# Stages ahead of an expert loop in another order: row tiles in banks of their own, products by which low parts they need, group sums inside the output projection

## The chip, the cores and the metric

The kernel runs on one core of one Trainium2 chip. Its metric is the device time of one execution in microseconds. The profiled execution is one more run of the same program, read by the hardware profiler.

## The reference

One layer of a decoder on 512 tokens of 1024 numbers, all in float32. Two token mixers, an attention in a sliding window and a short convolution, share one input projection; each result is normalised on its own, both go through one output projection, and a mixture of 32 experts (four for each token) follows.

```python
h = rmsnorm(x, g_mix)
p = h @ w_in                              # 768 columns q,k,v and 1536 of the convolution
attn = sliding_window_attention(q, k, v, sinks)      # 8 heads, blocks of 128 queries
conv = short_conv(b_gate, c_gate, x_in, conv_w)      # b * (width-3 conv of c * x_in)
mix = concatenate([rmsnorm(attn, g_attn_out), rmsnorm(conv, g_conv_out)])
x = x + mix @ w_out
h = rmsnorm(x, g_ffn)
x = x + moe(h, w_router, b_router, w1, b1, w2, b2)   # top 4 of 32, softmax gates
out = rmsnorm(x, g_final)
```

## The kernel before

The order of work is written out by hand: each engine has its own list of instructions, and semaphores tie them. The 512 tokens are `TB` = 4 row tiles of 128. Four stages follow each other.

**Input.** For each row tile ScalarE takes the sum of squares (`row_std`), VectorE scales the rows (`norm`), TensorE turns them (`turn_rows`), ScalarE rounds what was turned to the short float format of TensorE (`high_xn`, into `xnT_hi`), and VectorE keeps the rest (`low_xn`, into `xnT_lo`). The row tiles use two pairs of PSUM banks in turn. Weights are split in the same way, `high_tile` on ScalarE and `low_tile` on VectorE, a tile of 128 columns at a time.

**Projection and attention.** `project(m, bank, done)` makes one of 18 column tiles, six of q, k, v and then twelve of the convolution, from 24 products: for each of eight slices `k` high x high, high weight x low rows, low weight x high rows. Between them lie the scores, the turning of the probabilities and `attend(n)` for each of four blocks. VectorE's loop over the blocks ends with `attended(n)` (L955, L957), which scales the attention output and sums its squares. The last block also prepares the output weights: `high_w_out` (ScalarE L1414) and `low_w_out` (VectorE L981), eight slices in the order `W_OUT_EARLY + W_OUT_LATE`; `high_mix` (L1421, L1422) and `low_mix` (L987, L988) split the mixed rows of one row tile.

**Output projection.** `out_proj(t, n)` takes row tile `t` and column half `n`, 24 products (L634 to L636) into two banks, one of each group. `group_sums` (L645) adds the squares of both groups over the partitions; ScalarE takes the root (L1466), VectorE the reciprocal (L1060). Only then can `residual(t, n)` (L1068, L1069) scale the banks and add them to `X`, which frees them for row tile `t + 1`. `second_norm` (L1082), `turn_h2`, `router` and `rank` follow for each row tile, one tile behind.

**Experts.** SyncE streams all the weights of the experts through a ring of 16 slots of 1 MB. The first four slots are asked for once the last `project` is done, the next four once the output projection is, the third part once the rows of the first expert were fetched (`rows_in`), and all others as slots come free. TensorE multiplies at L778, L785, L804 and L810. Then the result rows are gathered and added (L1278) and normalised.

## Time and profile before

| | us |
|---|---|
| median of 3 runs | 1254.84 |
| lowest and highest | 1253.53, 1255.98 |
| the profiled execution | 1252.27 |
| its span, first to last instruction | 1250.5 |
| TensorE busy | 1158.2 (93%) |
| VectorE, ScalarE, GpSimd busy | 309.7, 198.1, 169.9 |
| mean bytes by DMA | 368 GB/s |

Times of the trace are microseconds from the start of the span. A row of the timeline gives the start, how long, the engine, the line, the operation with what it writes and reads, and in brackets how long the engine had been idle and who released it.
### The profile page before, as it was taken

The page shows a single profiled execution, that of the slowest core. Times are in us where ns is not written, and L with a number is a line of the kernel's source. Part 1 is how long each engine was busy: PE and PEld are TensorE (multiplying, and loading weights), DVE is VectorE, ACT ScalarE, POOL GpSimd, SP SyncE. Part 2 cuts the span into 40 slices and gives each one's busy share as a digit, 9 for nine tenths or more (in the row PEclk, how much of TensorE's full clock was granted, in tenths as well). Part 3 has the DMA queues.
Part 4 walks back from the last instruction along what each step waited for, and adds up shares of the span by engine and source line. Part 5 has one row for each costly group of instructions (what it writes and reads, how often), then busy time and mean ns, then how long its engine had stood idle before and what let it go on. Part 6 is the DMA issues. An engine that isn't in the chain of part 4 may idle for free. (4 is left out here: it accounts for less than half of the span.)

```text
span 1250.5 us, 16597 instructions
## 1 busy us (share of the span) xinstructions
PE 1158.2 (93%) x7030; PEld 484.9 (39%) x7030; DVE 309.7 (25%) x470; ACT 198.1 (16%) x385; POOL 169.9 (14%) x246
## 2 busy tenths in 40 slices
PE   5999998798999999999999898999989899998980
PEld 4777677323333333333333333333333333333330
DVE  4678855411101202101101010110101011010108
ACT  4453623001001101011010000101000010100002
POOL 6000000341111201111111011111101111111000
PEclk9999989698999999999999999999999999999995
DMA  9400635999999999999999999999999999999996
GB/s 332 145 1 27 236 142 220 320 392 411 423 424 424 423 425 423 425 422 425 424 423 425 425 423 424 425 423 423 424 424 424 423 425 423 424 423 424 425 394 249
DMA packets 59246, 460.67 MB, mean 368 GB/s; under 512 B 12438, under 2 KB 12710, under 8 KB 26306
## 3 DMA queue, kind: packets, MB, share of 16 engines
q1 hardware_dynamic: 49362, 434.15, 84.0%
q0 software_dynamic: 7632, 17.05, 3.6%
q10 hardware_dynamic: 2176, 8.39, 1.7%
q8 instruction: 57, 0.93, 0.3%
q14 instruction: 19, 0.16, 0.0%
HBM read 442.58 MB, written 21.41 MB: 371 GB/s over the span
## 5 line engine op out<-in xcount | busy, mean ns | idle before, releaser
L778 PE MATMUL ps<-ring_a,blockT 128*64 128x512 f32 x1472 | 327.2, 595 | 15.6 <-DMA ring_a<-in_w 15.5
L1234 DVE TENSOR_SCALAR xnT<-ps 128x768 f32<-128x768 f32 (+1 forms) x32 | 26.9, 841 | 828.4 <-PE ps L785 520.6
L778 PEld LDWEIGHTS ps<-ring_a,blockT 128*64 128x64 f32 x1472 | 101.1, 137 | 226.8 <-issue 187.7
L804 PE MATMUL ps<-ring_a,actT 128*64 128x512 f32 x736 | 166.3, 598 | 0.0
L1497 ACT ACTIVATE blockT<-ps 128x512 f32<-128x512 f32 x30 | 17.9, 597 | 561.4 <-PE ps L730 561.4
L778 PE MATMUL ps<-ring_b,blockT 128*64 128x512 f32 x448 | 99.7, 595 | 6.7 <-DMA ring_b<-in_w 6.7
L1674 POOL DMA_INDIRECT scores<-h_rows,slots x30 | 31.7, 1058 | 509.6 <-PE ps L730 508.7
L785 PE MATMUL ps<-ring_a,blockT 128*32 128x512 f32 x768 | 87.4, 595 | 0.0
L804 PEld LDWEIGHTS ps<-ring_a,actT 128*64 128x64 f32 x736 | 50.2, 137 | 93.5 <-issue 91.0
L1690 POOL DMA_INDIRECT expert_rows<-normed,slots x32 | 32.9, 1029 | 270.1 <-ACT normed L1526 269.8
L804 PE MATMUL ps<-ring_b,actT 128*64 128x512 f32 x288 | 64.7, 596 | 0.0
L524 PE MATMUL ps<-xnT_hi,ring_r 128*128 128x512 f32 x144 | 57.8, 401 | 5.6 <-DVE ring_r L892 3.5
L778 PEld LDWEIGHTS ps<-ring_b,blockT 128*64 128x64 f32 x448 | 30.7, 137 | 71.0 <-issue 57.3
L525 PE MATMUL ps<-xnT_lo,ring_r 128*128 128x512 f32 x144 | 56.9, 395 | 0.0
L526 PE MATMUL ps<-xnT_hi,ring_r 128*128 128x512 f32 x144 | 56.8, 394 | 0.0
L810 PE MATMUL ps<-ring_a,actT 128*32 128x256 f32 x832 | 50.3, 382 | 0.0
L785 PEld LDWEIGHTS ps<-ring_a,blockT 128*32 128x32 f32 x768 | 22.5, 109 | 62.6 <-issue 62.6
L1255 DVE TENSOR_TENSOR xnT<-xnT 128x768 f32<-128x768 f32 (+1 forms) x32 | 42.7, 1334 | 9.3 <-ACT xnT L1520 8.7
L810 PEld LDWEIGHTS ps<-ring_a,actT 128*32 128x32 f32 x832 | 24.4, 109 | 34.5 <-issue 21.1
L1525 ACT ACTIVATE normed<-ps,slots 128x256 f32<-128x256 f32 x18 | 8.5, 474 | 174.5 <-PE ps L810 174.5
L1526 ACT ACTIVATE normed<-ps,slots 128x512 f32<-128x512 f32 x32 | 21.9, 684 | 81.8 <-PE ps L804 81.8
L804 PEld LDWEIGHTS ps<-ring_b,actT 128*64 128x64 f32 x288 | 20.0, 136 | 35.9 <-issue 35.0
(289 smaller groups left out, 1090.3 us busy)
## 6 DMA issues: line engine op xcount, KB each, us to landing
ring_a<-in_w SPq DMA_DIRECT2D x98, 2048.0 KB, 32.1
ring_a<-in_w SPq DMA_DIRECT2D x92, 1024.0 KB, 30.1
ring_b<-in_w SPq DMA_DIRECT2D x30, 2048.0 KB, 31.0
ring_b<-in_w SPq DMA_DIRECT2D x36, 1024.0 KB, 32.8
ring<-in_w_in SPq DMA_DIRECT2D x12, 768.0 KB, 19.2
ring<-expert_rows SPq DMA_DIRECT2D x16, 512.0 KB, 14.7
h_rows<-normed ACTq DMA_DIRECT2D x4, 1536.0 KB, 6.5
X<-in_x SPq DMA_DIRECT2D x8, 512.0 KB, 6.1
```

The lines of the kernel that those rows point to most:

```text
L524: mm(ps[:, bank, :], high[:, k, :], xnT_hi[:, k, :], start=(k == 0), stop=False)
L525: mm(ps[:, bank, :], high[:, k, :], xnT_lo[:, :, k, :], start=False, stop=False)
L526: ins = mm(ps[:, bank, :], low[:, k, :], xnT_hi[:, k, :], start=False, stop=(k == KT - 1))
L778: ins = mm(ps[half * HALF:(half + 1) * HALF, b, :], x_of(k)[0], ring(r)[:, 0, at + half * 512:at + (half + 1) * 512], start=False, stop=(k ...
L785: mm(ps[q * QUARTER:(q + 1) * QUARTER, B_BOTH, :], x_of(k)[1], w[:, :, q * 256:(q + 1) * 256], start=False, stop=(k == KT - 1), tile_posit ...
L804: ins = mm(ps[half * HALF:(half + 1) * HALF, bank, :], actT[:, s % 2 * W2_K + j, s // 2 * HALF:(s // 2 + 1) * HALF], ring(r)[:, 0, j * D + ...
L810: ins = mm(ps[q * QUARTER:(q + 1) * QUARTER, bank + 1, 0:256], actT[:, 4 + j, s * QUARTER:(s + 1) * QUARTER], ring(slot(s)[0])[:, 0, j * D ...
L1234: v.tensor_scalar(width(glu_c, big), width(ps_glu, big), LIMIT, None, ALU.min).then_inc(glu_ready, 1)
L1255: v.tensor_tensor(turned.rearrange("p (s k q) -> p s q k", k=W2_K, q=P), a_in.rearrange("p (s q k) -> p s q k", k=W2_K, q=P), b_in.rearran ...
L1526: a.activation(gated_y[:, parity, 0:512], ps[:, bank, :], ACT.Copy, scale=gates[:, HALVES, 1:2].bitcast(F32)).then_inc(y_ready, 1)
L1674: g.indirect_dma_start(gathered[:, 0:512], None, h2_halves, bass.IndirectOffsetOnAxis(lists[:, HALVES, 0:1], 0), bounds_check=last_half_ro ...
L1690: g.indirect_dma_start(y_halves, bass.IndirectOffsetOnAxis(slots[:, HALVES, i, 0:1], 0), gated_y[:, parity, 0:512], None, bounds_check=las ...
```

## The change

Six edits, none in the expert loop.

1. The four row tiles are turned into four pairs of banks (`2 * t` in place of `2 * (t % 2)`), and TensorE no longer waits for `xn_lo` between them. ScalarE takes the sums of squares of three row tiles before the first `high_xn`.
2. `project` waits for the high weights, makes all eight high x high products, then the eight with the low rows, and waits for the low weights only ahead of the last eight.
3. The first output tile is made by `out_first` in the same manner, for both halves; `group_sums` stands ahead of its last 16 products, those with the low weights.
4. VectorE no longer makes two low slices of `w_out` inside the last block; after the block comes `low_mix(0)`, then two slices, `attended(3)`, four slices, `low_mix(1)`.
5. The sum of the squares of the convolution over its four channel tiles goes from one reduction on VectorE (L1055) to three additions on GpSimd, each as its square arrives.
6. `out_proj` keeps the old product order for row tiles 1 to 3.

TensorE's first projected tile, in the order of the program before; `tile_lo` is told by VectorE:

```order
L506 MATMUL ps<-ident,normed 128x128 [waits xn_lo,xn_ready]
L506 MATMUL ps<-ident,normed 128x128 x7
L524 MATMUL ps<-xnT_hi,ring_r 128x512 [waits tile_lo,xn_lo]
L525 MATMUL ps<-xnT_lo,ring_r 128x512
L526 MATMUL ps<-xnT_hi,ring_r 128x512
```

The same place in the changed program:

```order
L505 MATMUL ps<-ident,normed 128x128 [waits xn_ready]
L505 MATMUL ps<-ident,normed 128x128 x7
L521 MATMUL ps<-xnT_hi,ring_r 128x512 [waits tile_hi,xn_lo,xn_hi]
L521 MATMUL ps<-xnT_hi,ring_r 128x512 x7
L525 MATMUL ps<-xnT_lo,ring_r 128x512 [waits xn_lo]
L525 MATMUL ps<-xnT_lo,ring_r 128x512 x7
L528 MATMUL ps<-xnT_hi,ring_r 128x512 [waits tile_lo]
L528 MATMUL ps<-xnT_hi,ring_r 128x512 x7
```

The wait for the low weights has moved behind sixteen products.

TensorE at the end of the first output tile, before; the three rows of products ahead of the sums are the last of 48:

```order
L634 MATMUL ps<-ring_r,xnT_hi 128x512
L635 MATMUL ps<-ring_r,xnT_hi 128x512
L636 MATMUL ps<-ring_r,mixer_r 128x512
L645 MATMUL ps<-ones_col,early 128x1 [waits csqs_ready,osqs_ready]
L645 MATMUL ps<-ones_col,early 128x1 x7
L634 MATMUL ps<-ring_r,xnT_hi 128x512 [waits x2_half,mix_lo]
```

And the whole of it in the changed program, from the last `attend`:

```order
L587 MATMUL ps<-probsT,mixer 64x256 x7
L637 MATMUL ps<-ring_r,xnT_hi 128x512 [waits mix_hi,wout_hi,conv_read,u_ready]
L637 MATMUL ps<-ring_r,xnT_hi 128x512 [waits wout_hi] x7
L642 MATMUL ps<-ring_r,mixer_r 128x512 [waits mix_lo]
L642 MATMUL ps<-ring_r,mixer_r 128x512 x7
L637 MATMUL ps<-ring_r,xnT_hi 128x512 x8
L642 MATMUL ps<-ring_r,mixer_r 128x512 x8
L670 MATMUL ps<-ones_col,early 128x1 [waits csqs_ready,osqs_ready]
L670 MATMUL ps<-ones_col,early 128x1 x3
L670 MATMUL ps<-ones_col,normed 128x1 x4
L649 MATMUL ps<-ring_r,xnT_hi 128x512 [waits wout_lo] x8
L649 MATMUL ps<-ring_r,xnT_hi 128x512 x8
```

The sums stand ahead of sixteen products where they stood behind all of them.

VectorE from the end of the last block's `attended(2)` to the first `residual`, before:

```order
L957 TENSOR_REDUCE early<-early 128x128
L981 TENSOR_TENSOR ring_r<-ring,ring_r 128x1024 [waits wout_hi] x2
L1034 TENSOR_TENSOR early<-early,ps 128x512 [waits part_done]
L1043 COPY probsT<-ps 128x512 [waits dve_step,pv_done,probs_turned]
L1046 TENSOR_SCALAR mixer<-early,g_conv 128x512
L1043 COPY probsT<-ps 128x512 [waits probs_turned]
L981 TENSOR_TENSOR ring_r<-ring,ring_r 128x1024 [waits wout_hi]
L987 TENSOR_TENSOR mixer_r<-mixer,xnT_hi 128x4x128 [waits mix_hi]
L988 TENSOR_TENSOR mixer_r<-mixer,xnT_hi 128x4x128
L981 TENSOR_TENSOR ring_r<-ring,ring_r 128x1024 [waits wout_hi] x3
L955 TENSOR_TENSOR mixer<-ps,g_attn 128x4x128 [waits osq_ready]
```

And in the changed program:

```order
L980 TENSOR_REDUCE early<-early 128x128
L1053 TENSOR_TENSOR early<-early,ps 128x512 [waits part_done]
L1062 COPY probsT<-ps 128x512 [waits dve_step,pv_done,probs_turned]
L1065 TENSOR_SCALAR mixer<-early,g_conv 128x512
L1062 COPY probsT<-ps 128x512 [waits probs_turned]
L1010 TENSOR_TENSOR mixer_r<-mixer,xnT_hi 128x4x128 [waits mix_hi]
L1011 TENSOR_TENSOR mixer_r<-mixer,xnT_hi 128x4x128
L1004 TENSOR_TENSOR ring_r<-ring,ring_r 128x1024 [waits wout_hi] x2
L978 TENSOR_TENSOR mixer<-ps,g_attn 128x4x128 [waits osq_ready]
L980 TENSOR_REDUCE early<-early 128x128
L1004 TENSOR_TENSOR ring_r<-ring,ring_r 128x1024 [waits wout_hi] x4
```

Two slices have left the place ahead of the block's last multiplication, and six are now made behind `low_mix(0)`. The diff, cut to its core:

```diff
-                if t >= 2:
-                    pe.wait_ge(xn_lo, 2 * (t - 1))
-                turn_rows(normed[:, t % 2, :], 2 * (t % 2)).then_inc(xn_turned, 1)
+                turn_rows(normed[:, t % 2, :], 2 * t).then_inc(xn_turned, 1)
...
-                pe.wait_ge(tile_lo, m + 1)
+                pe.wait_ge(tile_hi, m + 1)
                 _, low, high = weight_tile(m)
                 for k in range(KT):
                     mm(ps[:, bank, :], high[:, k, :], xnT_hi[:, k, :], start=(k == 0), stop=False)
+                if m == 0:
+                    pe.wait_ge(xn_lo, 2 * TB)
+                for k in range(KT):
                     mm(ps[:, bank, :], high[:, k, :], xnT_lo[:, :, k, :], start=False, stop=False)
+                pe.wait_ge(tile_lo, m + 1)
+                for k in range(KT):
                     ins = mm(ps[:, bank, :], low[:, k, :], xnT_hi[:, k, :], start=False, stop=(k == KT - 1))
...
-            pe.wait_ge(xn_lo, 2 * TB)
+            pe.wait_ge(xn_hi, 2 * TB)
+            pe.wait_ge(xn_lo, 2 * (TB - 1))
...
+            def out_first():
+
+                pe.wait_ge(u_ready, CT)
+                pe.wait_ge(conv_read, CT)
+                for n in range(2):
+                    if n == 0:
+                        pe.wait_ge(mix_hi, 1)
+                    for order, k in enumerate(W_OUT_EARLY + W_OUT_LATE):
+                        if n == 0:
+                            pe.wait_ge(wout_hi, order + 1)
+                        bank, high, _, w_high, _ = out_parts(0, n, k)
+                        mm(bank, high, w_high, start=(k in (0, W_OUT_LATE[-1] + 1)), stop=False)
+                    if n == 0:
+                        pe.wait_ge(mix_lo, 1)
+                    for k in W_OUT_EARLY + W_OUT_LATE:
+                        bank, _, low, w_high, _ = out_parts(0, n, k)
+                        mm(bank, low, w_high, start=False, stop=False)
+                group_sums()
+                for n in range(2):
+                    for order, k in enumerate(W_OUT_EARLY + W_OUT_LATE):
+                        if n == 0:
+                            pe.wait_ge(wout_lo, order + 1)
+                        bank, high, _, _, w_low = out_parts(0, n, k)
+                        ins = mm(bank, high, w_low, start=False, stop=(k in (CT - 1, W_OUT_LATE[-1])))
+                    ins.then_inc(oproj_done, 1)
...
-            out_proj(0, 0)
-            out_proj(0, 1)
-            group_sums()
+            out_first()
...
-                if n == TB - 1:
-                    low_w_out(2)
-                    low_w_out(3)
-
...
-            for order in range(4, KT):
+            low_mix(0)
+            for order in range(2, KT):
                 low_w_out(order)
-                if order == 4:
-                    low_mix(0)
-            attended(TB - 1)
-            dve.wait_ge(sq_ready, CT)
-            v.tensor_reduce(conv_sqs[:, :], conv_sq.rearrange("p c t -> p t c"), AX_X, ALU.add).then_inc(csqs_ready, 1)
+                if order == 3:
+                    attended(TB - 1)
             low_mix(1)
...
-                if t >= 1:
-                    high_xn(t - 1)
-            high_xn(TB - 1)
+                if t >= 2:
+                    high_xn(t - 2)
+            for t in range(TB - 2, TB):
+                high_xn(t)
...
+            for n in range(1, CT):
+                pool.wait_ge(sq_ready, n + 1)
+                ins = g.tensor_tensor(conv_sq[:, 0, :], conv_sq[:, 0, :], conv_sq[:, n, :], ALU.add)
+                if n < CT - 1:
+                    then(ins)
+                else:
+                    ins.then_inc(csqs_ready, 1)
```

## Rows read from the trace of the kernel before

**Rows 1.** The page's 40 slices of the span: bytes moved by DMA.

```profile
GB/s 332 145 1 27 236 142 220 320 392 411 423 424 424 423 425 423 425 422 425 424 423 425 425 423 424 425 423 423 424 424 424 423 425 423 424 423 424 425 394 249
```

**Rows 2.** The windows view: stretch, length, busy time of five engines, PEclk, DMA share, GB/s.

```profile
430.00:530.00 100.00, 100.00 (x646) 34.09 (x644) 14.15 (x18) 10.08 (x19) 14.11 (x14) 1.00 1.01 424
730.00:830.00 100.00, 95.53 (x578) 31.23 (x578) 11.81 (x14) 8.98 (x17) 12.80 (x12) 1.00 1.01 424
```

**Rows 3.** Timeline of SyncE's queue: requests for experts' weights.

```profile
146.81 85.57 SPq L417 DMA_DIRECT2D ring_a<-in_w  x6
```

**Rows 4.** Timeline of TensorE where the first expert's rows have come.

```profile
231.69 1.51 PE L723 MATMUL ps<-ident,scores 96*128 96x96 f32 x8 [0.61 <-DMA scores<-h_rows,tok_static]
```

**Rows 5.** Timeline of TensorE at the first projected tile.

```profile
22.51 0.77 PE L524 MATMUL ps<-xnT_hi,ring_r 128*128 128x512 f32 x1 [3.47 <-DVE ring_r L892]
```

**Rows 6.** Timeline of ScalarE there.

```profile
19.08 1.08 ACT L1346 ACTIVATE xnT_hi<-ps 128x512 fp32r<-128x512 f32 x2 [1.59 <-PE ps L506]
20.05 2.00 ACT L1340 ACTIVATE ring_r<-ring 128x1024 fp32r<-128x1024 f32 x2
```

**Rows 7.** Timeline of VectorE there.

```profile
21.14 2.36 DVE L892 TENSOR_TENSOR ring_r<-ring,ring_r 128x1024 fp32r<-128x1024 f32 x2
```

**Rows 8.** Timeline of TensorE from the third block's attention to the second row tile.

```profile
131.14 1.95 PE L584 MATMUL ps<-probsT,mixer 128*64 128x256 f32 x16
...
144.03 1.03 PE L567 MATMUL ps<-ident,scores 128*128 128x128 f32 x8
145.32 0.66 PE L567 MATMUL ps<-ident,scores 128*128 128x128 f32 x4 [0.25 <-ACT probsT L1451]
147.46 0.66 PE L567 MATMUL ps<-ident,scores 128*128 128x128 f32 x4 [1.48 <-DVE probsT L1043]
148.94 3.35 PE L584 MATMUL ps<-probsT,mixer 128*64 128x256 f32 x16 [0.83 <-issue]
152.22 0.73 PE L634 MATMUL ps<-ring_r,xnT_hi 128*128 128x512 f32 x1
...
163.49 1.84 PE L645 MATMUL ps<-ones_col,early 128*128 128x1 f32 x16
167.59 0.77 PE L634 MATMUL ps<-ring_r,xnT_hi 128*128 128x512 f32 x1 [2.26 <-DVE X L1069]
...
175.78 1.03 PE L506 MATMUL ps<-ident,normed 128*128 128x128 f32 x8
```

**Rows 9.** The windows view in that stretch, columns as in Rows 2.

```profile
150.00:151.00 1.00, 1.00 (x8) 0.74 (x6) 1.00 (x2) 1.00 (x3) 0.00 (x0) 0.50 1.03 422
169.00:170.00 1.00, 1.00 (x4) 0.80 (x3) 0.96 (x2) 0.00 (x0) 0.00 (x0) 0.50 0.00 0
```

**Rows 10.** Timeline of VectorE in that stretch.

```profile
143.44 2.35 DVE L981 TENSOR_TENSOR ring_r<-ring,ring_r 128x1024 fp32r<-128x1024 f32 x2
145.71 0.68 DVE L1034 TENSOR_TENSOR early<-early,ps 128x512 f32<-128x512 f32 x1
148.15 0.69 DVE L1043 COPY probsT<-ps 128x512 f32<-128x512 f32 x1 [0.36 <-PE ps L567]
...
151.09 3.49 DVE L981 TENSOR_TENSOR ring_r<-ring,ring_r 128x1024 fp32r<-128x1024 f32 x3
...
156.11 3.80 DVE L1055 TENSOR_REDUCE early<-normed 128x512 f32<-128x2048 f32 x1
...
165.91 0.75 DVE L1068 SCALAR_TENSOR_TENSOR X<-ps,r_group,X 128x512 f32<-128x512 f32 x1
...
171.83 1.42 DVE L1082 SCALAR_TENSOR_TENSOR normed<-X,stat,gain_ffn 128x512 f32<-128x512 f32 x2
```

**Rows 11.** Timeline of ScalarE in that stretch.

```profile
149.10 2.93 ACT L1414 ACTIVATE ring_r<-ring 128x1024 fp32r<-128x1024 f32 x3
```

**Rows 12.** The views of single lines: GpSimd L1606, then VectorE L885.

```profile
L1606 POOL TENSOR_SCALAR ring<-ring x8: 849/852/1832, 4.3 to 12.7; 128x256 f32<-128x256 f32 x8
...
L885 DVE SCALAR_TENSOR_TENSOR normed<-X,stat,gain_a x4: 1283/1285/1285, 7.0 to 15.7; 128x1024 f32<-128x1024 f32 x4
```

More of the change, by code:

```diff
@@ L231, in layer_kernel @@
         u_pad = early[:, 3 * SEQ:]
-        conv_sqs = u_pad[:, 0:SEQ]
         upper = scores[:, HEADS // 2:, :].rearrange("p h s -> p (h s)")
@@ L613, in _, with out_parts @@
                     scores_of(n + 1, 1)
+            def out_parts(t, n, k):
+                half, c = k // CT, k % CT
+                rows, cols = slice(t * P, (t + 1) * P), slice(n * 512, (n + 1) * 512)
+                return (ps[:, 2 * n + half, :], mixT_hi[:, k, rows], (attnT_lo, convT_lo)[half][:, c, rows],
+                        w_out_hi[:, W_OUT_PLACES[k], cols], w_out_lo[:, k, cols])
+            def out_first():
[22 more added lines that the diff above has]
+                    ins.then_inc(oproj_done, 1)
@@ L616, in out_proj @@
             def out_proj(t, n):
-                if t == 0 and n == 0:
-                    pe.wait_ge(u_ready, CT)
-                if t == 0 and n == 1:
-                    pe.wait_ge(conv_read, CT)
                 if n == 0:
                     pe.wait_ge(mix_lo, t + 1)
-                if t:
-                    pe.wait_ge(x2_half, 2 * (t - 1) + n + 1)
-                cols = slice(n * 512, (n + 1) * 512)
-                for order, k in enumerate(W_OUT_EARLY + W_OUT_LATE):
-                    if t == 0 and n == 0:
-                        pe.wait_ge(wout_lo, order + 1)
-                    half, c = k // CT, k % CT
-                    bank = ps[:, 2 * n + half, :]
-                    high, low = mixT_hi[:, k, t * P:(t + 1) * P], (attnT_lo, convT_lo)[half][:, c, t * P:(t + 1) * P]
-                    w_high = w_out_hi[:, W_OUT_PLACES[k], cols]
+                pe.wait_ge(x2_half, 2 * (t - 1) + n + 1)
@@ L634, in out_proj @@
+                for k in W_OUT_EARLY + W_OUT_LATE:
+                    bank, high, low, w_high, w_low = out_parts(t, n, k)
                     mm(bank, high, w_high, start=(k in (0, W_OUT_LATE[-1] + 1)), stop=False)
-                    mm(bank, high, w_out_lo[:, k, cols], start=False, stop=False)
+                    mm(bank, high, w_low, start=False, stop=False)
                     ins = mm(bank, low, w_high, start=False, stop=(k in (CT - 1, W_OUT_LATE[-1])))
@@ L642, in group_sums @@
                 pe.wait_ge(csqs_ready, 1)
-                for half, src in enumerate((attn_sqs, conv_sqs)):
+                for half, src in enumerate((attn_sqs, conv_sq[:, 0, :])):
                     for t in range(TB):
@@ L898, in low_xn @@
                     half = slice(4 * b, 4 * b + 4)
-                    v.tensor_tensor(xnT_lo[:, t, half, :], ps[:, 2 * (t % 2) + b, :].rearrange("p (k t) -> p k t", k=4),
+                    v.tensor_tensor(xnT_lo[:, t, half, :], ps[:, 2 * t + b, :].rearrange("p (k t) -> p k t", k=4),
                                     xnT_hi[:, half, t * P:(t + 1) * P].bitcast(F32), ALU.subtract).then_inc(xn_lo, 1)
@@ L1345, in high_xn @@
                 for b in range(2):
-                    a.activation(xnT_hi[:, 4 * b:4 * b + 4, t * P:(t + 1) * P], ps[:, 2 * (t % 2) + b, :].rearrange("p (k t) -> p k t", k=4),
+                    a.activation(xnT_hi[:, 4 * b:4 * b + 4, t * P:(t + 1) * P], ps[:, 2 * t + b, :].rearrange("p (k t) -> p k t", k=4),
                                  ACT.Copy).then_inc(xn_hi, 1)
```

## The prediction

> **What bounds the kernel now.** I read the page's slices first. The DMA engines move 423 to 425 GB/s in nearly every slice from the eleventh on, and next to nothing in the third [rows 1]. The windows view of the expert loop says the same from both sides: in the stretch from 430 us TensorE is busy for all of 100 us and DMA moves 424 GB/s, in the one from 730 us TensorE is busy for 95.5 us and DMA again moves 424 GB/s [rows 2]. So the loop is a stream of weights at the full rate, and its length is its bytes over that rate. The diff touches neither. What it can move is the moment at which the stream begins. SyncE's queue asks for only the first eight slots before that: six requests for `ring_a` are spread over 85.57 us from 146.81 on, and the last two of these come after `rows_in` [rows 3]. TensorE turns the first expert's rows at 231.69, freed by the fetch of these rows [rows 4]. The fetch needs the routing of the last row tile, which comes from TensorE's own chain through the stages before. So the question is what TensorE waits for, and how fast it runs, ahead of 231.69. A microsecond saved there should be one saved at the end. I then read TensorE's timeline for gaps, and the granted clock behind each.
>
> **The start: 1.3 us.** TensorE's first projected product starts at 22.51, freed by VectorE's low weight tile after 3.47 us of idling [rows 5]. VectorE makes two such tiles in 2.36 us from 21.14 on [rows 7], so the first costs some 1.2 us plus the handing over. Its high tile is the first of two that ScalarE makes in 2.00 us from 20.05 [rows 6], done at 21.1. The changed program needs only that one: 22.51 - 21.15 = 1.36 us. The low rows of the last row tile are needed eight products later and the low weights sixteen later; both are done by 22.4, and eight products take at least 1.9 us, so these waits end unseen. The banks of their own bring nothing by themselves: the last row tile's scaling on VectorE starts at 15.7 and takes 1.285 us [rows 12], TensorE turns it, and ScalarE's copies start at 19.08 [rows 6]. VectorE has no room ahead of it, and the earlier sums of squares on ScalarE now stand ahead of the first `high_xn`. I take 0.1 us off for that (0 to 1 us lost, if the third row tile of `x` lands late, since ScalarE now waits for it ahead of `high_xn(0)`). The other bound is the pace at the start: the first product takes 0.77 us [rows 5], as does the first one at half clock later on [rows 8]. If the pace rises no earlier than before, products started 1.36 us sooner run at half pace for that long and bring 0.7. Sum: 1.3 us, between 0 and 1.4. The other seventeen tiles have the same 24 products each and no gap to win.
>
> **The end of attention.** In the last block VectorE makes two low slices of `w_out` from 143.44 on for 2.35 us, and only then, at 145.71, the product L1034 [rows 10], whose input TensorE finished by about 144.2, when it went on to turn probabilities (144.03) [rows 8]. Everything to `attend(3)` hangs on that: TensorE idles 1.48 us until 147.46, then 0.83 us until 148.94 [rows 8]. With the slices gone L1034 starts 1.5 us sooner. TensorE is free for the last turning at 145.32 + 0.66 = 145.98, so that moves from 147.46 to 146.0, and `attend(3)` from 148.94 to 147.5. It took 3.35 us there, and the same sixteen took 1.95 us one block before [rows 8]: the granted clock was 0.50 [rows 9], the lower of its two levels, after three microseconds in which TensorE had mostly idled. With 1.5 us less of idling I expect 1.00 and 1.95 us, so that it ends at 149.45 in place of about 152.2.
>
> **A new wait eats part of it.** `out_first` needs all eight high slices of `w_out` in its first eight products. ScalarE makes the last three of them from 149.10 for 2.93 us, to 152.03 [rows 11]. That chain doesn't move. Before, three products lay between two slices and hid it. Now the eighth product would start at about 151.3 and has to wait 0.8 us, until 152.1. The clock's gain of 1.4 us in `attend(3)` therefore mostly goes into this wait.
>
> **The sums in the middle: the largest term.** Before, 48 products ran from 152.22 to 163.49, 0.235 us each; then the sums took 1.84 us; then TensorE idled 2.26 us for root, reciprocal and first `residual`, and started the second row tile at 167.59 [rows 8]. After: from 152.1 on 41 products at 0.235 and the sums, 152.1 + 9.6 + 1.8 = 163.6. Sixteen products (3.8 us) lie behind the sums, and the first eight of them close the banks of half 0 at about 161.7; root and reciprocal are long done by then. `residual(0, 0)` takes two operations of 0.75 us [rows 10] and ends at 163.2, so TensorE goes on at 163.6 without a gap: 167.59 - 163.6 = 4.0 us. The 24 products of `out_proj(1, 0)` took 175.78 - 167.59 = 8.19 us [rows 8] at a granted clock of 0.50 [rows 9] over most of it. At 0.235 us they take 5.6: another 2.55 us. What is late next is `turn_h2(0)`: VectorE ended the second norm at 171.83 + 1.42 = 173.25, 7.3 us behind the start of the first `residual` at 165.91 [rows 10]. From 161.7 that gives 169.05, just ahead of TensorE at 163.6 + 5.6 = 169.2. So the turn moves from 175.78 to 169.2, 6.6 us, with nothing to spare. From there the order is the old one and the rest moves as it is.
>
> **What hides the moved work.** VectorE's chain from `low_mix(0)` on starts when ScalarE has the rows, 149.2: 1.2 us, two slices at 1.2, `attended(3)` 1.6, four slices 4.7, `low_mix(1)` 1.2, end near 160.2; one slice is a third of 3.49 [rows 10]. The last slice is ready at about 159.0 and needed at 161.5; `low_mix(1)` is done 1.5 us ahead of `residual(0, 0)`. The reduction of 3.80 us at 156.11 [rows 10] would not have fitted; it is now three additions on GpSimd. No row shows such an addition. The nearest is L1606, one input of half the length, 0.85 us undisturbed [rows 12]: twice that is the least, 1.7 us, four times the most, 3.4. The last square arrives at 147.2, so the addition ends by 150.6, and the sums need it at 158. Nothing on the path: zero, and 0.6 us at worst if it had to wait for a pause of VectorE. Queued behind it on GpSimd are only the clearing of the row buffer and small constants, needed far later.
>
> **Trace and rule.** Of L1606's eight operations some took 1.83 us in place of 0.85, beside VectorE's L885, while L885 stayed between 1.283 and 1.285 us all four times, three of them beside GpSimd's work [rows 12]. VectorE lost nothing. The Trainium skill (SBUF — State Buffer, section Who interferes with whom) says that a VectorE instruction with two SBUF inputs and a GpSimd one that reads SBUF lock each other out, whichever comes second. The trace agrees for GpSimd, not for VectorE. By that rule `low_mix(0)` could wait for the addition: a rival below.
>
> **Sum.** 1.3 + 6.6 = 7.9 us. The profiled execution took 1252.27 us, which gives 1244.4; it lies 2.57 us under the median of the runs shown. Taken from the median: 1254.84 - 7.9 = **1246.9 us**.
>
> **The rivals.** (a) *The clock stays low.* `attend(3)` still starts at 0.50 and the first products with it: 3.35 us from 147.5, then seven products at 0.43, so the eighth starts at 153.9 and not 152.1, 1.8 us lost; and the clock could fall behind the sums as it did before, now inside `out_first`, 2.55 us more, the price at that place in [rows 8]. Against it: the idling is 1.5 us shorter, and the gap behind the sums is gone. 1248.7, at most 1251.3. (b) *GpSimd holds VectorE.* The addition runs from 147.3 to 150.6, `low_mix(0)` starts 1.4 us late, all the slack of VectorE's chain goes, and the rest lands on the first `residual` and on `turn_h2(0)`: 0.4 to 1 us, 1247.6. For it is only the slowing of L1606; against it L885. (c) *Slower: the grouped products cost more each.* 432 products of the projection and 48 of the first output tile now run in groups of eight from the same kind of operand; before, kinds alternated. If the alternation hid weight loads or reads that groups don't, each costs more. From 7.9 / 480 = 16 ns each (0.235 to 0.251) the kernel is slower than before; at twice that 1262.7. Nothing in the rows speaks for a difference between the kinds. (d) *The loop doesn't pass it on.* If the stream began by something else than `rows_in`, or lost at its start what it won, the time would stay at 1254.8. Against it: the queue's rows show the requests held back until 232 [rows 3].
>
> **How the numbers follow.** Forecast 0.60, (a) 0.22, (b) 0.06, (c) 0.04, (d) 0.08. The forecast's own case spans 1244.2 (runs of one kernel differ by over 1 us to either side) to 1248.5 (no gain at the start). With (a) up to two thirds of its price the range goes to 1250.4; beyond lie (c), (d) and the tail. A difference of 0.2%, 2.5 us, is about what can be told from none. Faster by over that: forecast, (a), (b), 0.88; within it: (d), 0.08; slower: (c), 0.04.
>
> **What would show it.** In the changed profile: first projected product near 21.2 and not 22.5; no wait of the last turning of probabilities; sixteen products of `attend(3)` in 2 and not 3.4 us; a wait of some 0.8 us for ScalarE's L1414 (its new number) inside the first output tile; the second row tile started with no gap, some 5.3 us sooner, at clock 1.00; the turning of the first expert's rows near 223.8; and the loop's length from there as before. If that last moves by other than the end does, the first step of this text is wrong.

## The result, and the profile after

The changed kernel takes 1248.11 us (median of 5 runs, 1244.19 to 1248.85). The kernel before took 1255.98 us in the 5 runs beside them, the three shown above among these. The ratio is 0.9933, 95% interval 0.9919 to 0.9947: faster by 0.7%, 8.4 us (6.7 to 10.2). Two later timings of the same pair gave 0.9927 (0.991 to 0.9945) and 0.9912 (0.9899 to 0.9925). The forecast was 1246.9 us, range 1244.2 to 1250.4.

The two profiled executions lie closer together: 1252.27 us before, 1248.85 after. So these two traces hold only 3.4 us of the difference.

TensorE's timeline after, at the first projected tile and the next; the columns are as before:

```profile
20.98 3.75 PE L521 MATMUL ps<-xnT_hi,ring_r 128*128 128x512 f32 x8 [2.21 <-ACT ring_r L1357]
24.53 3.09 PE L525 MATMUL ps<-xnT_lo,ring_r 128*128 128x512 f32 x8
27.46 2.00 PE L528 MATMUL ps<-xnT_hi,ring_r 128*128 128x512 f32 x8
29.29 1.98 PE L521 MATMUL ps<-xnT_hi,ring_r 128*128 128x512 f32 x8
31.11 1.98 PE L525 MATMUL ps<-xnT_lo,ring_r 128*128 128x512 f32 x8
```

It starts 1.53 us sooner than in [rows 5] and waits for ScalarE's high tile only. But the first eight products take 3.55 us (24.53 - 20.98), 0.44 each, where the eight from 29.29 take 1.82, 0.228 each. The second tile starts at 29.29; before it started at 29.90, so 0.61 of the 1.53 us are left there.

The same view around the last block of attention and the first output tile, against [rows 8]:

```profile
145.00 1.03 PE L570 MATMUL ps<-ident,scores 128*128 128x128 f32 x8
146.28 1.32 PE L570 MATMUL ps<-ident,scores 128*128 128x128 f32 x8 [0.25 <-ACT probsT L1469]
148.44 1.95 PE L587 MATMUL ps<-probsT,mixer 128*64 128x256 f32 x16 [0.83 <-ACT probsT L1469]
...
152.03 0.50 PE L637 MATMUL ps<-ring_r,xnT_hi 128*128 128x512 f32 x1
152.97 0.50 PE L637 MATMUL ps<-ring_r,xnT_hi 128*128 128x512 f32 x1 [0.44 <-ACT ring_r L1432]
...
159.58 1.03 PE L670 MATMUL ps<-ones_col,normed 128*128 128x1 f32 x8
160.48 3.93 PE L649 MATMUL ps<-ring_r,xnT_hi 128*128 128x512 f32 x16
164.37 0.47 PE L659 MATMUL ps<-ring_r,xnT_hi 128*128 128x512 f32 x1
...
170.08 1.09 PE L505 MATMUL ps<-ident,normed 128*128 128x128 f32 x8
```

The last turning no longer waits (one row of eight in place of two of four), `attend(3)` takes 1.95 and not 3.35 us, the eighth product stands 0.94 us behind the seventh (0.7 over the usual 0.235: the new wait), and the second row tile follows at once. From the first of these rows to the last it is 25.08 us; before it was 31.75.

VectorE there, against [rows 10], and the line of GpSimd's additions:

```profile
145.20 0.69 DVE L1053 TENSOR_TENSOR early<-early,ps 128x512 f32<-128x512 f32 x1 [0.21 <-PE ps L528]
150.10 0.69 DVE L1010 TENSOR_TENSOR mixer_r<-mixer,xnT_hi 128x512 fp32r<-128x512 f32 x1 [1.77 <-ACT xnT_hi L1440]
162.68 0.75 DVE L1085 SCALAR_TENSOR_TENSOR X<-ps,r_group,X 128x512 f32<-128x512 f32 x1 [1.53 <-PE ps L649]
168.61 1.41 DVE L1099 SCALAR_TENSOR_TENSOR normed<-X,stat,gain_ffn 128x512 f32<-128x512 f32 x2
```
```profile
L1673 POOL TENSOR_TENSOR normed<-normed x3: 1277/1286/1302, 103.5 to 148.2; 128x512 f32<-128x512 f32 x3
```

VectorE has 1.53 us to spare ahead of the first `residual`. What did not go well stands elsewhere, near 60 us. The windows view there, then the turning of the first expert's rows, against [rows 4], and SyncE's queue behind it, against [rows 3]:

```profile
62.00:63.00 1.00, 1.00 (x4) 0.81 (x3) 1.00 (x2) 1.00 (x2) 0.00 (x0) 0.50 0.00 0
```
```profile
60.50 3.36 PE L521 MATMUL ps<-xnT_hi,ring_r 128*128 128x512 f32 x8 [2.17 <-DVEq L998]
...
226.11 1.51 PE L746 MATMUL ps<-ident,scores 96*128 96x96 f32 x8 [0.66 <-DMA scores<-h_rows,tok_static]
```
```profile
226.00 0.81 SPq L416 DMA_DIRECT2D ring_a<-in_w  x2
226.84 1.48 SPq L416 DMA_DIRECT2D ring_b<-in_w  x2
240.83 3.41 SPq L421 DMA_DIRECT2D ring_a<-in_w  x4
```

At 62 us the granted clock is 0.50, which the trace of before does not have there, and the 24 products from 60.50 take 7.18 us where before they took 5.59: 1.6 us lost. The rows are turned 5.58 us sooner, and the stream goes on with them.

### The profile page after: what moved, and what is told of

It reads as the page before. It is cut to its first block and busy times, and to the rows that moved or that the text cites. A ratio compares the mean times of both kernels' runs of the same rounds, so it can differ in the third digit from the quotient of the medians.

```text
span 1247.3 us, 16600 instructions
## 1 busy us (share of the span) xinstructions
PE 1159.8 (93%) x7030; PEld 483.9 (39%) x7030; DVE 306.2 (25%) x469; ACT 197.6 (16%) x385; POOL 172.3 (14%) x249
## 5 line engine op out<-in xcount | busy, mean ns | idle before, releaser
L1251 DVE TENSOR_SCALAR xnT<-ps 128x768 f32<-128x768 f32 (+1 forms) x32 | 26.9, 841 | 830.8 <-PE ps L808 522.8
L521 PE MATMUL ps<-xnT_hi,ring_r 128*128 128x512 f32 x144 | 39.6, 421 | 4.4 <-ACT ring_r L1357 2.2
L525 PE MATMUL ps<-xnT_lo,ring_r 128*128 128x512 f32 x144 | 37.1, 401 | 0.0
L528 PE MATMUL ps<-xnT_hi,ring_r 128*128 128x512 f32 x144 | 35.6, 389 | 0.0
```

The source lines that it names most:

```text
L521: mm(ps[:, bank, :], high[:, k, :], xnT_hi[:, k, :], start=(k == 0), stop=False)
L525: mm(ps[:, bank, :], high[:, k, :], xnT_lo[:, :, k, :], start=False, stop=False)
L528: ins = mm(ps[:, bank, :], low[:, k, :], xnT_hi[:, k, :], start=False, stop=(k == KT - 1))
L1251: v.tensor_scalar(width(glu_c, big), width(ps_glu, big), LIMIT, None, ALU.min).then_inc(glu_ready, 1)
```

## Where an execution spends its time

Each profiled kernel is one execution. Three distances in TensorE's timeline, and what is left to the end of the span, put all fourteen side by side (us; the last column says whether the clock fell near 60 us):

| kernel | turning of the last block's probabilities at | from there to `turn_h2(0)` | to the rows of the first expert | from there to the end | 0.50 near 60 us |
|---|---|---|---|---|---|
| before | 144.03 | 31.75 | 55.91 | 1018.8 | no |
| old_again (the kernel before) | 144.21 | 32.01 | 55.79 | 1022.3 | no |
| after | 145.00 | 25.08 | 56.03 | 1021.2 | yes |
| again (changed) | 144.84 | 25.09 | 55.82 | 1023.3 | yes |
| again_2 (changed) | 142.31 | 25.08 | 56.25 | 1022.6 | no |
| sums_last | 143.95 | 28.49 | 55.65 | 1022.4 | yes |
| slices_early | 142.68 | 29.70 | 55.84 | 1020.9 | no |
| low_first | 146.29 | 25.13 | 55.61 | 1022.5 | yes |
| squares_on_vector | 144.28 | 27.33 | 56.08 | 1022.5 | yes |
| rows_later | 142.70 | 25.09 | 61.14 | 1020.8 | no |
| rows_much_later | 144.70 | 25.09 | 67.41 | 1019.9 | yes |
| warm_start | 140.53 | 25.08 | 55.99 | 1022.2 | no |
| warm_tail | 142.36 | 25.09 | 55.21 | 1021.0 | no |
| warm_all | 140.04 | 25.09 | 55.50 | 1021.6 | no |

The second column repeats to 0.01 us in the three executions of the changed kernel. In the two of the kernel before it is 0.26 us apart: there stretches of the lower clock lie inside it, and VectorE's chain stood otherwise to TensorE's, so that the last turning waited 2.08 us in `old_again` where it waited 1.48:

```profile
148.24 0.66 PE L567 MATMUL ps<-ident,scores 128*128 128x128 f32 x4 [2.08 <-DVE probsT L1043]
```

So an edit that brings no low clock into this column can be read from one execution; one that does can't be read to better than about a microsecond. Between executions of one kernel the first column moved by up to 2.7 us, the last by up to 3.5. Three things stand behind that.

*The moment at which the clock rises at the start.* In the second control, `again_2`, TensorE's timeline has the same first product as after, but the pace is full by 24.5 and not by 26.9:

```profile
21.04 3.62 PE L521 MATMUL ps<-xnT_hi,ring_r 128*128 128x512 f32 x8 [2.21 <-ACT ring_r L1357]
24.50 2.01 PE L525 MATMUL ps<-xnT_lo,ring_r 128*128 128x512 f32 x8
...
28.16 1.98 PE L521 MATMUL ps<-xnT_hi,ring_r 128*128 128x512 f32 x8
```

The Trainium skill (TensorE: Matmul & The Clock Gate, Part 1, on the warm-up) says that the number of slow products at a kernel's start differs from run to run, because the gate's observation of activity is not tied to the program's start. The traces agree: the second tile starts at 28.16 here and at 29.29 in after.

*The fall near 60 us.* The gap ahead of it, 2.17 us for VectorE, is the same in every execution without added products ahead of it. The clock fell behind it in six of ten such executions of the changed order, in two of the three of the changed kernel itself, and in neither of the two of the kernel before. So the changed order doesn't bring the fall each time, as `again` alone could have suggested; whether it makes the fall likelier is open, since two executions of the kernel before are too few to tell. The windows view of `again_2`, where it did not:

```profile
62.00:63.00 1.00, 1.00 (x6) 0.80 (x6) 0.85 (x3) 0.98 (x2) 0.00 (x0) 1.00 0.00 0
```

*The first expert.* In `old_again`, the kernel before once more, TensorE idles three times, 3.4 us in all, inside the first expert's products, with nothing that the trace shows to wait for:

```profile
257.43 1.30 PE L785 MATMUL ps<-ring_a,rowsT 128*32 128x512 f32 x3 [0.82 <-issue]
260.25 1.05 PE L785 MATMUL ps<-ring_a,rowsT 128*32 128x512 f32 x3 [1.52 <-issue]
262.37 4.69 PE L785 MATMUL ps<-ring_a,rowsT 128*32 128x512 f32 x22 [1.07 <-issue]
```

The profiled executions of before and of after have no such row; the twelve others do, with 1.9 to 4.4 us in all. The profiled execution of before has the shortest loop of all fourteen, 1018.8 us, against 1022.3 in `old_again`: 3.5 of the 3.8 us between the two executions (1252.27 and 1256.05), where the kernel's medians are 1256 to 1258. The idling alone doesn't explain it: after has none either, and its loop is 2.4 us longer than that of before. Why it comes and goes is open.

## The experiments

Ratios are to the kernel before, run on the same chip; 0.001 is 1.26 us. The experiments ran in three sets. The changed kernel's own ratios were 0.9927 in the first (`again`) and 0.9912 in the third (`again_2`). The second set (`low_first`, `squares_on_vector`, `rows_later`, `warm_start`) ran on another chip than these two, with no run of the changed kernel beside it, so its distances are given against both ratios; against the ratio of the result, 0.9933, the costs would be another 0.8 us smaller and the gain as much larger.

**again, old_again, again_2: both kernels unchanged.**

> The changed kernel once more. In its first profile the last project tile ended to the first turning of the second row tile in 25.1 us (31.8 before), as forecast, but TensorE ran at half clock from 60.5 to about 64.5, where before it had not, and the first expert's rows were turned only 5.6 us sooner. Theory 1 (the granted clock at that place differs from run to run of one and the same kernel): in this profile the stretch from 60 to 64 may be at full clock, the rows are turned near 224, and the ratio to the kernel before is again 0.992 to 0.995. Rival (the new order of products, or what surrounds it, lowers the clock there): half clock from 60 to 64 again, rows near 226.

> The kernel before once more, one look. Theory 1: full or half clock at 60 to 64 us by chance, the half clock behind the group sums and in the last block's attend again in most runs, the time within 1253 to 1258. Rival: full clock at 60 to 64, as in its first profile, since only the changed kernel is slowed there.

> The changed kernel once more, as it is, beside the three others of this set: their control. Both theories: about 0.993 of the kernel before (1249.4 us in its last timing). The first expert's rows are turned at about 226 us. If the fall of the granted clock near 60 us belongs to this order and not to one execution, TensorE runs at 0.50 there again: it did in five of the seven profiled executions of kernels of this order without added products, and in neither of the two of the kernel before.

Measured: `again` 1249.44 us, 0.9927 (0.991 to 0.9945); `old_again` 1256.05 us, one run; `again_2` 1247.52 us, 0.9912 (0.9899 to 0.9925). The gain repeats, and so does the second column of the table. The clock at the start of `old_again`, in the windows view, is the lower level to about 26.6 us, which the records of before don't show although its products there took as long:

```profile
24.00:26.00 2.00, 2.00 (x6) 1.52 (x6) 0.00 (x0) 0.00 (x0) 0.12 (x1) 0.50 1.02 416
26.00:28.00 2.00, 2.00 (x9) 1.66 (x8) 0.00 (x0) 0.00 (x0) 0.00 (x0) 0.85 1.02 418
```

**sums_last: the group sums behind the whole first output tile again, all else changed.**

```diff
-                group_sums()
                 for n in range(2):
...
                     ins.then_inc(oproj_done, 1)
+                group_sums()
```

> The changed kernel with the group sums behind all 48 products of the first output tile, as before. Theory (the sums in the middle hide root, reciprocal and first residual, 2.3 us, and keep the clock up, 2.5 us): slower than the changed kernel by 4 to 5 us, about 0.9965 to 0.998 of the kernel before; in the profile an idle gap of 2.3 us ahead of the second row tile and half clock for most of its first 24 products. Rival (the gap matters, the clock would stay up): slower by 2.3 us, clock 1.00 there.

Measured: 1252.51 us, 0.9959 (0.994 to 0.9977), 4.0 us over `again` by the ratios, 3.1 by the medians; the intervals just touch. TensorE's timeline behind the sums, and a window in the tile that follows:

```profile
162.15 1.03 PE L670 MATMUL ps<-ones_col,normed 128*128 128x1 f32 x8
165.44 0.76 PE L659 MATMUL ps<-ring_r,xnT_hi 128*128 128x512 f32 x1 [2.26 <-DVE X L1086]
...
168.54 0.39 PE L660 MATMUL ps<-ring_r,xnT_hi 128*128 128x512 f32 x1
```
```profile
166.00:167.00 1.00, 1.00 (x4) 0.80 (x3) 1.00 (x2) 0.00 (x0) 0.00 (x0) 0.50 0.06 16
```

The idling of 2.26 us is back, to the hundredth as in [rows 8], and with it the lower clock. The second column grows by 3.41 us, not by the 4 to 5 that were expected. The lower clock was back for a shorter time: the pace is full again at 168.54, after seven products, where in the kernel before it took thirteen. The 24 products of this tile took 7.00 us (8.19 before, 5.71 in the changed kernel). With the clock of before the place of the sums would be worth 3.41 + 1.19 = 4.6 us, an estimate from these rows.

**slices_early: the two low slices of `w_out` inside the last block again.**

```diff
+                if n == TB - 1:
+                    low_w_out(2)
+                    low_w_out(3)
...
-            for order in range(2, KT):
+            for order in range(4, KT):
```

> The changed kernel with VectorE making two low slices of w_out inside the last block again, ahead of its last multiplication. Theory (the slices hold up the last turning of probabilities by 1.5 us, of which ScalarE's high slices take 0.4 back): slower than the changed kernel by 1.0 us, 2.5 us if attend(3) also falls to half clock; the wait for the last high slice (0.44 us) gone. Rival (what ScalarE makes sets the first output tile whatever VectorE does): within 0.3 us of the changed kernel.

Measured: 1254.56 us, 0.9973 (0.9962 to 0.9985), 5.8 us over `again` by the ratios, 5.1 by the medians; the second column 4.62 us longer, where 1.0 to 2.5 were expected. TensorE's, VectorE's and GpSimd's timelines:

```profile
146.10 0.66 PE L570 MATMUL ps<-ident,scores 128*128 128x128 f32 x4 [1.48 <-DVE probsT L1066]
149.13 3.68 PE L587 MATMUL ps<-probsT,mixer 128*64 128x256 f32 x16 [2.38 <-issue]
152.74 3.05 PE L637 MATMUL ps<-ring_r,xnT_hi 128*128 128x512 f32 x8
```
```profile
145.35 0.69 DVE L1066 COPY probsT<-ps 128x512 f32<-128x512 f32 x1 [0.32 <-DVE early L1057]
145.96 2.48 DVE L1069 TENSOR_SCALAR mixer<-early,g_conv 128x512 f32<-128x512 f32 x1
148.36 0.67 DVE L1066 COPY probsT<-ps 128x512 f32<-128x512 f32 x1
```
```profile
145.99 1.27 POOL L1677 TENSOR_TENSOR normed<-normed 128x512 f32<-128x512 f32 x1 [20.76 <-ACT normed L1476]
147.20 0.96 POOL L1684 MEMSET scores<- 128x1024 f32 x1
```

The wait of 1.48 us and the half pace of `attend(3)` are as before. But there is a new cost: VectorE's scaling L1069 takes 2.48 us in place of 0.48 (the other three), and it spans GpSimd's addition and the clearing behind it, 145.99 to 148.16. In the changed kernel the same scaling starts at 146.81 and the last addition at 148.2, so they miss each other. So the rival of the prediction, GpSimd holding VectorE, can happen, as far as one trace shows: in the other ten executions with these additions the third one starts 0.9 us behind the scaling's end, and the scaling takes 0.48. It struck another instruction than the one named. Behind the longer wait the lower clock also lasts longer: the eight products from 152.74 take 2.89 us. The Trainium skill (SBUF — State Buffer, section Who interferes with whom) says that copies and `tensor_scalar` between SBUF operands can take the port pair that VectorE shares with GpSimd, and that whoever issues first gets it for the whole instruction while the other is blocked. The trace agrees that one of the two waits: VectorE paid 2.0 us. On the order it doesn't: the scaling is recorded at 145.96, 0.03 us ahead of the addition, and it is the one that paid; the records may not tell so small a distance.

**low_first: the projection waits for the low weights ahead of all 24 products.**

```diff
-                pe.wait_ge(tile_hi, m + 1)
+                pe.wait_ge(tile_lo, m + 1)
...
-                pe.wait_ge(tile_lo, m + 1)
```

> The changed kernel, but every projected tile waits for its low weights ahead of its first product, as before; the grouped order stays. Theory (TensorE's first product starts 1.4 us sooner by the high weights alone): first product near 22.4 and not 21.0, and slower than the changed kernel by 0.7 to 1.4 us. Rival (the pace of the first products rises at the same moment in any case, and the gain is half): 0.7 us. Second rival (the row tiles' own banks brought part of it): first product before 22.2.

Measured: 1251.03 us, 0.9938 (0.9921 to 0.9955): 1.4 or 3.3 us over the changed kernel, by which of its ratios is taken. The interval overlaps those of the changed kernel, so by the time alone no cost is shown. Its first product starts at 22.50, as in [rows 5], 1.5 us later than in the changed kernel, and the second tile starts 1.2 us behind that of after (30.53 against 29.29), and 1.2 to 2.4 us behind those of the nine executions with the changed start:

```profile
22.50 3.75 PE L521 MATMUL ps<-xnT_hi,ring_r 128*128 128x512 f32 x8 [3.72 <-DVE ring_r L914]
...
30.53 1.98 PE L521 MATMUL ps<-xnT_hi,ring_r 128*128 128x512 f32 x8
```

The second column is that of the changed kernel, so the edit works through this one tile. That the first product is back at 22.50 also rules out the second rival: the row tiles' own banks brought nothing here.

**squares_on_vector: the squares of the convolution summed on VectorE again, between the slices.**

```diff
+                    dve.wait_ge(sq_ready, CT)
+                    v.tensor_reduce(u_pad[:, 0:SEQ], conv_sq.rearrange("p c t -> p t c"), AX_X, ALU.add).then_inc(csqs_ready, 1)
...
-            for n in range(1, CT):
-                pool.wait_ge(sq_ready, n + 1)
-                ins = g.tensor_tensor(conv_sq[:, 0, :], conv_sq[:, 0, :], conv_sq[:, n, :], ALU.add)
```

> The changed kernel with the convolution's squares summed by one reduction on VectorE again, right behind attended(3). Theory (VectorE has only 1.7 us to spare between there and the first residual, by the profile of the changed kernel): the reduction's 3.8 us make the last low slices and low_mix(1) late, the first residual starts 2 to 2.5 us later, and the kernel is 2 to 3 us slower than the changed one. Rival (GpSimd's additions cost VectorE elsewhere, since a tensor_scalar of VectorE took 2.5 us in place of 0.5 beside one of them in the run before): no slower, or up to 1 us faster.

Measured: 1252.64 us, 0.9959 (0.9944 to 0.9973), 4.0 or 5.9 us over the changed kernel, where 2 to 3 were expected; the second column, 2.25 us longer, agrees with the expectation. VectorE's timeline, then TensorE's:

```profile
154.47 3.85 DVE L1074 TENSOR_REDUCE early<-normed 128x512 f32<-128x2048 f32 x1
158.24 4.62 DVE L1004 TENSOR_TENSOR ring_r<-ring,ring_r 128x1024 fp32r<-128x1024 f32 x4
```
```profile
158.47 1.92 PE L670 MATMUL ps<-ones_col,early 128*128 128x1 f32 x16 [0.24 <-DVE early L1074]
162.91 2.32 PE L649 MATMUL ps<-ring_r,xnT_hi 128*128 128x512 f32 x9 [0.63 <-DVE ring_r L1004]
165.89 0.47 PE L659 MATMUL ps<-ring_r,xnT_hi 128*128 128x512 f32 x1 [0.66 <-DVE X L1088]
```

Without the offload to GpSimd, the earlier sums would find VectorE full: TensorE waits for the sum, for a slice, and for the `residual`.

**rows_later and rows_much_later: 5 and 12 clearings of a buffer on GpSimd ahead of the first fetch of rows.**

```diff
             pool.wait_ge(tok_ready, 1)
+            for _ in range(5):
+                ins = g.memset(early[:, 0:D], 0.0)
+                then(ins)
             fetch(0)
```

> The changed kernel with five clearings of an unused buffer of 1024 columns on GpSimd, about 5 us, ahead of the fetch of the first expert's rows; nothing else on the path. Theory (the weights' stream starts with these rows and then runs at the full rate to the end, so a delay there arrives whole): slower than the changed kernel by 4.5 to 5.2 us. Rival (the loop's early part has slack between stream and TensorE, and swallows some of it): 0 to 3 us.

> Twelve clearings of a buffer (0.95 us each, 11.5 us in all) ahead of the first fetch of rows. Theory (the stream of weights begins when the rows come in, and the loop passes a delay on in full): the rows are turned some 12 us later than in the changed kernel, near 238, and the median is 11 to 12 us above the control's, about 1261. Rival (the loop has slack at its start and gives part of a delay back): five clearings cost the median only about 1.5 us of 5; by that share twelve would cost 4 to 6 us, about 1254.

Measured: `rows_later` 1250.98 us, 0.9943 (0.9926 to 0.9959), 2.0 or 3.9 us over the changed kernel, where 4.5 to 5.2 were expected and the rows came 5.1 us later (third column). `rows_much_later` 1257.97 us, 1.0005 (0.9996 to 1.0014), 11.7 us over the control of its set (10.5 by the medians), where the rows came 67.41 - 56.25 = 11.2 us later. TensorE in `rows_much_later`:

```profile
237.20 1.51 PE L746 MATMUL ps<-ident,scores 96*128 96x96 f32 x8 [10.62 <-DMA scores<-h_rows,tok_static]
```

Within its interval the large delay is passed on in full. The small one alone would have left that open, with no run of the changed kernel beside it.

**warm_start, warm_tail, warm_all: added products whose results are not used fill TensorE's waits, so that the clock stays up.** At the start (40 of them, and 8 ahead of the gap near 60 us), in the routing behind the second norm and the first expert, or both.

```diff
+            fill(12, 7)
             for t in range(TB):
...
+                    fill((5, 7, 5)[t], 7)
...
             ins.then_inc(vT_turned, 1)
+            fill(8, 7)
```

> The changed kernel with TensorE filled, wherever it idles up to the first projected product and in the idle time at 58 to 60 us, by products whose results nobody reads (12 before the first turning, 5, 7, 5 and 11 behind the four turnings, 8 at 58 us), so that the clock stays at 2.4 GHz. Theory (what the clock costs at the start is on the path): the turnings take 1.0 and not 2.0 us each, the first product starts about 0.9 us sooner, the first tile takes 5.5 and not 8.3 us, no half clock at 60 us: faster than the changed kernel by 3.5 to 5 us. Rival (the clock stays at its low level at the start, or the filling holds up real work): the same or slower.

> Extra products of 0.2 to 0.3 us each (their results unused) fill TensorE's waits in the routing behind the second norm and ahead of the second expert's turning. Theory (the lower level of the clock behind these waits is on the path up to the rows): router(3) takes 2.0 in place of 3.6 us, the turning of the rows 1.0 in place of 2.0, they come 2 to 3 us sooner, near 223.5, and the median is 2 to 4 us under the control's. Rival (from the rows on only the stream counts, and each added product that ends after its wait delays what follows): the rows come at most 0.5 us sooner, and the median is within 1 us of the control's.

> The extra products of warm_tail and those of warm_start together. If both act on the path, in different stretches, the gains add: 3.6 us (measured for the start alone) and 2 to 4 us (the theory for the tail), about 6 us under the control, 1243. If the tail's are worth nothing, the result is that of the start alone, about 1246.

Measured: `warm_start` 1245.85 us, 0.99 (0.9883 to 0.9916); `warm_tail` 1247.03 us, 0.992 (0.9906 to 0.9934); `warm_all` 1244.67 us, 0.9899 (0.9886 to 0.9912). TensorE in `warm_start`:

```profile
17.77 2.54 PE L513 MATMUL ps<-ones_bf 128*128 128x512 bf16 x11
20.83 2.06 PE L533 MATMUL ps<-xnT_hi,ring_r 128*128 128x512 f32 x8 [0.52 <-ACT ring_r L1370]
22.72 1.98 PE L537 MATMUL ps<-xnT_lo,ring_r 128*128 128x512 f32 x8
26.35 1.98 PE L533 MATMUL ps<-xnT_hi,ring_r 128*128 128x512 f32 x8
```

The first products run at full pace, the second tile starts at 26.35 and not 29.29, and the clock holds at 60 us. In the table the last block comes 4.5 us sooner than in after and 1.8 us sooner than in `again_2`, an execution that had escaped the fall. In time it is 1.5 or 3.4 us under the changed kernel, by which of its ratios is taken, where 3.5 to 5 were expected (and the first product 0.9 us sooner; it is 0.15); `warm_all`, with its control beside it, is 1.6 us under (2.9 by the medians), with overlapping intervals. Both lie under the changed kernel in their medians and 1% under the kernel before. That the start moves is shown by the traces; how much of it reaches the time is not.

The tail is another matter. TensorE's timeline in `warm_tail`, where the rows are turned, against the row at 226.11 above:

```profile
222.66 0.85 PE L759 MATMUL ps<-ident,scores 96*128 96x96 f32 x8 [1.12 <-DMA scores<-h_rows,tok_static]
```

The granted clock is 1.00 behind the norm but for 212 to 216 us, where it fell once more (in `again_2` it is 0.50 from 206 on), and the turning takes 0.85 in place of 1.51 us, yet the rows come only 1.0 us sooner (third column 55.21 against 56.25), and the time is the control's (0.992 and 0.9912). Between TensorE's short pieces lie VectorE and the fetch, which keep their length. The theory asked for 2 to 3 us here and fell. In `warm_all` the clock fell ahead of the turning, which took 1.51 us again.

## Why the prediction held, and where it did not

**The first step, a microsecond saved ahead of the rows is one at the end:** right, though the pair of traces alone speaks against it. The rows moved by 5.58 us and the end of the span by 3.2, which the last paragraph of the prediction had named as its refutation. What moved by itself is the loop, by 2.4 us, and it does so between executions of one kernel (1018.8 and 1022.3 for the kernel before). `rows_much_later` is the test without that noise: 11.2 us later at the rows, 10.5 to 11.7 in time. What was wrong is the sign that the text set for its refutation. It compares two single executions, and that of before had a loop shorter than its kernel's other one by 3.5 us; the text noted that this execution lay 2.57 us under the median without asking where. The time itself was rightly taken from the median, but of three runs, 1254.84; five gave 1255.98, later sets 1257 to 1258.

**The start, 1.3 us between 0 and 1.4:** the wait went as forecast (20.98; 21.2 was said). The value taken was too high for the profiled execution: the second tile starts at 29.29, which is the bound of 0.7 us that the text gave for a pace that rises no earlier. The range of 0 to 1.4 was too narrow: the rise moved between 24.5 and 26.9 us among executions, and `again_2` stood 1.7 us ahead of before by its first column. The case without any gain at the start was also added up wrong, 1248.5 where 1254.84 - 6.6 is 1248.2. Nowhere did the text allow for the clock falling again near 60 us, which took 1.6 us in six of ten executions. The two together put the first column of after 0.97 us behind before, with 1.53 us won at its first product. Over the nine executions with the changed start that column is 143.65 in the mean, over the two of before 144.12: 0.5 us won, not 1.3.

**The end of attention:** right in each term, in all three executions of the changed kernel. The distance from the first turning to `attend(3)` is 3.44 us (said: 3.47, before: 4.91), its products take 1.95 us (eight instructions, each counted twice, which the prediction calls sixteen products), and no clock fell. Rival (a) did not come.

**The new wait, 0.8 us:** measured 0.7 us of distance, 0.44 of idle time.

**The sums in the middle and `turn_h2(0)`, 6.6 us:** 31.75 - 25.08 = 6.67 (6.93 from `old_again`). The experiments split it roughly: `sums_last` gives 3.41 back, `slices_early` 4.62. From the last turning to `attend(3)` that kernel takes 3.03 us (149.13 - 146.10) where the kernel before took 1.48, so 1.55 us of the 4.62 come with GpSimd's hold on VectorE, which the kernel before did not have. Its clock also stayed low for longer: from `attend(3)` to the ninth product of the first tile it took 6.50 us (149.13 to 155.63), the kernel before 5.47. That leaves 2.0 us for the slices. With the 4.6 us for the sums at the clock of before this makes 6.6 of the 6.67. It is an estimate from single executions, and that the two parts add up is assumed.

**GpSimd's additions, 1.7 to 3.4 us each, hidden:** hidden, and 1.29 us each, under the least bound. Doubling for the length was the wrong scaling from [rows 12]: with twice the length and a second input the addition took only half as long again. That the end of the additions lay outside VectorE's scaling was luck of alignment, 0.9 us of it.

**Rival (b)** did not come in the changed kernel; in `slices_early` its mechanism came, at another instruction. **(c)** did not: eight grouped products take 1.82 us, 0.228 each, the pace of before. **(d)** did not: `rows_much_later` shows the loop passing the delay on.

**The size:** 7.9 us forecast, 8.4, 9.2 and 11 by the three ratios. The traces account for 6.7 us plus what the start brings, 0.5 in the mean and between -1 and +1.7 in single executions. That leaves 1 to 4 us that I can't place; the spread of the loop between executions of one kernel, 2 to 3.5 us, is as large, and the interval of each ratio is some 2 us to either side. So the mechanism of the large term is shown, while part of the nearness of 8.4 to 7.9 is luck: the start brought less than was said, and the unplaced part filled in.

## What to carry to other kernels

When a wait of one engine can be filled by reordering its own work, price the wait, and then the clock behind it: here the same 2.26 us of idling cost TensorE another 2.5 us in the products that followed in one execution, and 1.4 in another. Before a sum is set against a profiled execution, compare that execution with the median and ask which stretch was the shorter one. Work moved to an idle GpSimd was free here where no scaling of VectorE between SBUF operands started beside it, and in the one trace where one did, VectorE paid 2.0 us; so read both timelines at that place.

## What the runs showed of the hardware that was not expected

The same idle gap of TensorE (2.17 us near 60 us, the same work on both sides) was followed by a clock of 0.50 for about 3.5 us in some executions and not in others. The rise at the start came between 24.5 and 26.9 us with the same work ahead of it. Behind the same 2.26 us of idling the lower clock lasted for thirteen products in one execution (before) and for seven in another (`sums_last`). An addition of two 128 x 512 float32 inputs on GpSimd took 1.28 to 1.30 us, and beside one of them and the clearing behind it, a VectorE `tensor_scalar` between SBUF operands took 2.48 in place of 0.48 us (one trace). The first expert's products show 1.9 to 4.4 us of idling without a visible cause in twelve of fourteen executions.
